# Seven-product scheme from the third column pair on, in a four-layer decoder trunk on one core

## The reference

```
def _swiglu(x, w13, w2):
    h = x @ w13                       # (512, 1024) @ (1024, 2 * 2816)
    g, u = jnp.split(h, 2, axis=-1)
    return (jax.nn.silu(g) * u) @ w2  # (512, 2816) @ (2816, 1024)
```

## Time and profile before

| what | value |
|---|---|
| time, median of 3 runs | 2118.74 us (2118.0 to 2120.76) |
| profiled execution, its own time | 2117.91 us |
| profiled execution, span from first to last instruction | 2116.0 us |
| granted TensorE clock, mean | 0.997 |
| PE matmul busy | 2093.9 us, 99% of the span, 14232 instructions |
| DVE busy | 1497.5 us, 71% |
| ACT busy | 915.3 us, 43% |
| POOL busy | 581.3 us, 27% |

### The profile page before, as it was taken

One profiled execution on the slowest core, in us unless ns is written; L12 is line 12 of the kernel. 1 busy time (PEld: TensorE's weight loads), 2 busy tenths in 40 slices (PEclk: granted clock), 3 DMA queues, 4 the chain that ended last, 5 costly groups with the idle time before them and its releaser, 6 DMA issues.

```text
span 2116.0 us, 37240 instructions
## 1 busy us (share of the span) xinstructions
PE 2093.9 (99%) x14232; PEld 1847.2 (87%) x14233; DVE 1497.5 (71%) x2106; ACT 915.3 (43%) x1662; POOL 581.3 (27%) x403
## 2 busy tenths in 40 slices
PE   9999999999999899999999999999999999999998
PEld 7777899998888689999888899988887778999987
DVE  3788688884379979888635888863638868888634
ACT  3455444443345134454323454442335454444422
POOL 0000146650030004666300366610000002666200
PEclk9999999999999999999999999999999999999999
DMA  6211333333233023334522233433332122334421
GB/s 219 70 50 50 94 109 101 101 109 129 92 110 100 23 70 110 101 101 115 176 96 64 80 100 103 116 122 99 101 89 61 60 78 73 100 110 111 125 94 60
DMA packets 256804, 204.65 MB, mean 97 GB/s; under 512 B 6272, under 2 KB 235776, under 8 KB 256656
## 3 DMA queue, kind: packets, MB, share of 16 engines
q1 hardware_dynamic: 252976, 189.42, 30.1%
q0 software_dynamic: 3680, 13.17, 1.9%
HBM read 200.47 MB, written 2.10 MB: 96 GB/s over the span
## 4 chain that ended last, share of the span: by engine, by line
PE 96%; DVE 2%; DMA 1%; ACT 1%; issue 0%; POOL 0%; DVEq 0%; POOLq 0%; SPq 0%; ACTq 0%
PE ps L1520 17%; PE ps L1522 17%; PE ps L1521 17%; PE ps L1599 12%; PE ps L1600 12%; PE ps L1601 12%; PE ps L1826 2%; PE ps L1854 2%; PE ps L1985 2%; PE ps L1641 1%; PE ps L1839 1%; PE ps L1830 1%; PE ps L2076 0%; DMA raw<-in_w 0%; PE ps L1652 0%
## 5 line engine op out<-in xcount | busy, mean ns | idle before, releaser
L986 DVE TENSOR_TENSOR w_lo<-raw,w_hi 128x1024 fp32r<-128x1024 f32 x188 | 233.4, 1247 | 317.4 <-ACT w_hi L609 316.6
L609 ACT ACTIVATE w_hi<-raw 128x1024 fp32r<-128x1024 f32 x188 | 195.5, 1056 | 345.3 <-PE ps L1522 336.1
L1599 PE MATMUL ps<-t_hi,w_hi 128*128 128x256 f32 x1216 | 344.3, 283 | 0.0
L1600 PE MATMUL ps<-t_lo,w_hi 128*128 128x256 f32 x1216 | 344.2, 283 | 0.0
L1601 PE MATMUL ps<-t_hi,w_lo 128*128 128x256 f32 x1216 | 344.2, 283 | 0.0
L678 ACT ACTIVATE w_hi<-raw 128x512 fp32r<-128x512 f32 (+1 forms) x304 | 224.2, 737 | 264.2 <-PE ps L1601 249.3
L1520 PE MATMUL ps<-w_hi,a_hi 128*128 128x512 f32 x832 | 326.3, 392 | 0.2
L1522 PE MATMUL ps<-w_hi,a_lo 128*128 128x512 f32 x832 | 324.0, 389 | 0.0
L1521 PE MATMUL ps<-w_lo,a_hi 128*128 128x512 f32 x832 | 323.9, 389 | 0.0
L1428 DVE TENSOR_TENSOR w_lo<-raw,w_hi 128x512 fp32r<-128x512 f32 (+1 forms) x304 | 281.6, 927 | 50.1 <-ACT w_hi L678 50.1
L1599 PE MATMUL ps<-xT_hi,w_hi 128*128 128x256 f32 x912 | 258.3, 283 | 0.0
(11 more groups left out here) (174 smaller groups left out, 4141.2 us busy)
## 6 DMA issues: line engine op xcount, KB each, us to landing
raw<-in_w SPq DMA_DIRECT2D x264, 512.0 KB, 4.0
raw<-in_wqkv SPq DMA_DIRECT2D x48, 512.0 KB, 3.7
raw<-in_pw SPq DMA_DIRECT2D x24, 512.0 KB, 4.3
raw<-in_wo SPq DMA_DIRECT2D x16, 512.0 KB, 3.4
ln_gb<-in_g POOLq DMA_DIRECT2D x8, 512.0 KB, 4.4
ln_gb<-in_b POOLq DMA_DIRECT2D x8, 512.0 KB, 5.7
x_nat<-in_x SPq DMA_DIRECT2D x4, 512.0 KB, 5.6
out<-x_nat SPq DMA_DIRECT2D x3, 512.0 KB, 2.6
```

The costliest lines, as they stand in the source:

```text
L609: nc.scalar.activation(weight_hi(u), raw[:, r, :], ACT.Copy).then_inc(w_hi_done, 1)
L986: nc.vector.tensor_tensor(weight_lo(u), raw[:, r, :], weight_hi(u).bitcast(f32), ALU.subtract).then_inc(w_lo_done, 1)
L1599: ms = [nc.tensor.matmul(dst, hi[:, at], x_hi, start=k == 0 and f in ("A11", "S1", "S2"), stop=False, skip_group_check=True), nc.tensor.ma ...
L1600: nc.tensor.matmul(dst, hi[:, at], x_lo, start=False, stop=False, skip_group_check=True),
```

## The change

Four things change, in each of the four stages "up".

1. `SEVEN_FROM` goes from 3 to 2. Pair 2 is no longer a plain pair, the scheme covers pairs 2 to 21 (20 of 22). On PE 48 matmuls over 512 tokens go and 84 over 256 tokens come.
2. On PE the first product, A11 of p = 0, is put ahead of unit 3, the last plain unit. Then come A12, S2, S1, S3.
3. `keep_first(0)` waits for unit 3 too, since its buffer lies in that unit's slot.
4. The low parts of the token sums are awaited one by one: S2 needs the first written (T2), S1 the second (T1), S3 the third (T3), A22 the fourth (T4). Before, S2 waited for all four. DVE and ACT make them in that order, with the splits of p = 0 between them; the fourth token sum is in a function of its own (`last_sum`).

```
-SEVEN_FROM, SEVEN_TO = 3, FC
+SEVEN_FROM, SEVEN_TO = 2, FC
...
-            order += [(p, f) for f in ("A11", "S2", "A12", "S1", "S3")]
+            order += [(p, f) for f in ("A11", "A12", "S2", "S1", "S3")]
...
                 act.wait_ge(form_used, used(i, p, "A11"))
+                if p == 0:
+                    act.wait_ge(w_used, u0 + 2 * SEVEN_FROM)
...
-                for k in range(AHEAD + 1, 2 * SEVEN_FROM):
-                    split_w(u0 + k)
+                split_w(u0 + AHEAD + 1)
+                form_high(0, G_A1)
                 activated(0)
+                form_high(0, G_S23)
+                for r in range(3):
+                    turned_hi(r)
+                keep_first(0)
+                form_high(0, G_S1)
                 activated(1)
...
-            split_w(u0 + 2 * SEVEN_FROM - 1)
-            for r in range(4):
-                turned_lo(r)
-            form_low(0, G_A1)
...
+            tokens_whole()
+            form_low(0, G_A1)
+            token_sums()
+            form_low(0, G_S23)
+            turned_lo(T2)
+            turned_lo(T1)
+            form_low(0, G_S1)
             gating(0)
-            token_sums()
...
+            turned_lo(T3)
+            make_u2(0)
+            last_sum()
+            gating(1)
             form_low(0, G_A22)
             form_low(0, G_S4)
...
+            turned_lo(T4)
...
                 elif f == "S2":
-                    pe.wait_ge(t_lo_done, 4 * (i + 1))
+                    pe.wait_ge(t_lo_done, 4 * i + 1)
...
-                for c in range(2, SEVEN_FROM):
-                    pair(c)
                 order = form_order()
-                for p, f in order[:-2]:
+                product(*order[0])
+                up_unit(u0 + AHEAD + 1, bank + AHEAD + 1)
+                for p, f in order[1:-2]:
                     product(p, f)
```

More of the change, by code:

```diff
@@ L700, in up @@
             if bias is None:
-                for k in range(AHEAD + 1, 2 * SEVEN_FROM):
-                    split_w(u0 + k)
+                split_w(u0 + AHEAD + 1)
+                form_high(0, G_A1)
                 activated(0)
-                activated(1)
-                for r in range(4):
[L706 to L709, removed]
+                form_high(0, G_S23)
[3 more added lines that the diff above has]
+                form_high(0, G_S1)
+                activated(1)
                 form_high(0, G_A22)
                 form_high(0, G_S4)
-                form_high(0, G_S1)
-                keep_first(0)
+                turned_hi(3)
                 first_tokens(0)
@@ L1397, in token_sums @@
             def token_sums():
-                r22, r12, r11, r21 = (t_raw[:, r, :, :] for r in range(4))
+                r22, r12, r11 = (t_raw[:, r, :, :] for r in range(3))
                 dve.wait_ge(t_raw_done, 4 * i + 2)
@@ L1405, in token_sums, with last_sum @@
                 nc.vector.tensor_tensor(r11, r22, r11, ALU.add).then_inc(t_sum_done, 1)
+            def last_sum():
+                r11, r21 = (t_raw[:, r, :, :] for r in (2, 3))
                 dve.wait_ge(t_raw_done, 4 * i + 4)
@@ L1469, in _ @@
             split_w(u0 + AHEAD + 1)
[L1470 to L1475, removed]
-            gating(0)
-            token_sums()
-            split_w(u0 + 2 * SEVEN_FROM - 1)
-            for r in range(4):
-                turned_lo(r)
-            form_low(0, G_A1)
-            gating(SEVEN_FROM - 2)
-            form_low(0, G_S23)
+            tokens_whole()
[5 more added lines that the diff above has]
+            form_low(0, G_S1)
+            gating(0)
+            turned_lo(T3)
+            make_u2(0)
+            last_sum()
+            gating(1)
             form_low(0, G_A22)
             form_low(0, G_S4)
-            gating(SEVEN_FROM - 1)
-            form_low(0, G_S1)
-            make_u2(0)
+            turned_lo(T4)
             for p in range(1, SEVENS):
@@ L1561, in up @@
                 up_columns(u0 + k, bank + k, second_half(b)).then_inc(w_used, 1)
-            up_unit(u0 + AHEAD + 1, bank + AHEAD + 1)
             X, Y, Z = seven_bank(i), seven_bank(i) + 1, seven_bank(i) + 2
@@ L1582, in product @@
                 elif f == "S2":
-                    pe.wait_ge(t_lo_done, 4 * (i + 1))
+                    pe.wait_ge(t_lo_done, 4 * i + 1)
                     if p:
                         pe.wait_ge(c21_done, m)
-                elif f == "S1" and p:
-                    pe.wait_ge(c12_done, m)
+                elif f == "S1":
+                    pe.wait_ge(t_lo_done, 4 * i + 2)
+                    if p:
+                        pe.wait_ge(c12_done, m)
                 elif f == "S3":
+                    pe.wait_ge(t_lo_done, 4 * i + 3)
                     pe.wait_ge(u2_done, m + 1)
                 elif f == "A22":
+                    pe.wait_ge(t_lo_done, 4 * (i + 1))
                     pe.wait_ge(u3_done, m + 1)
```

## The result

The changed kernel takes 2151.02 us (median of 4 runs, 2150.06 to 2153.0), the kernel before 2118.91 in the same session (4 runs, 2118.0 to 2120.76). The ratio is 1.0155, with a 95% interval of 1.0143 to 1.0168: 1.55% slower, where 2148 us (1.4%) was forecast. The profiled execution took 2150.42 us, its span is 2148.6 us, the mean granted clock 0.994 (2117.91, 2116.0 and 0.997 before).

The account below looks back on a forecast made before the run. PE bounds the kernel with DVE right behind in each stage head; a layer loses 7.7 + 0.6 - 0.82 - 0.1 = 7.35 us, four 29.4, on 2117.9 gives 2147.3, shown as 2148 us; range 2138 to 2160.

Parts of the forecast that it names:

- DVE's list: Stage head, layer 0: DVE's instructions up to the low part for A11 of p = 1 end at 292.3 us.
- the count of seven meetings: Stage head: seven POOL instructions take turns with DVE instructions having both inputs in SBUF, 1.07 us each, 7.5 in all.
- The waits: Stage head: PE loses 7.7 us a layer, at A11, A12, S1, S3 and A11 of p = 1.
- The wait at S3 of p = 1: Second scheme pair: DVE late once more, at `make_u2` before S3, 0.6 us a layer (0 to 0.7).
- The gain: PE, pair 2: a seven-product pair takes 10.08 us instead of 10.90, saving 0.82 a layer, 3.3 over four.
- the likeliest case: Whole kernel: DVE's list makes PE wait in each stage head, no clock fall; 2148 us, 1.4% slower, 77 in 100.
- the rival that had it at 15 in 100: Clock falls in the new hole, about 2 us after the last matmul; 1.5 us a layer, 2154; 15 in 100.
- against it: the holes sit between dense products: Argument against the clock falling: small transposes stood ahead of the convolution's stop, dense products surround the new 3.8 us hole.
- The sum: A layer: 7.7 + 0.6 - 0.82 - 0.1 = 7.35 us; four layers 29.4.
- Not slower: Stage head: POOL turns cost nothing, DVE's list ends at 284.8, A11 of p = 1 on time; 2118; 4 in 100.
- Lateness in every pair: All 20 scheme pairs: `make_u2` stays 0.6 us late, 46 us more, 2193; 4 in 100.
- Signs named ahead: New profile: A11 1.2 us late, 0.7 idle around unit 3, 3 to 4 at DVE's low part, period 10.08.

Follow-up runs that it names:

- experiment 6: Changed kernel with POOL's first three weight sums of a stage started earlier, ahead of the last tokens' low part; 2143.16 us, ratio 1.0112.
- experiment 3: Changed kernel with S2 ahead of A12 again on PE (A11, unit 3, S2, A12, S1, S3); 2152.27 us, ratio 1.0155.
- experiment 5: Changed kernel with T3's low part made twice on DVE, one more 128x1024 instruction in each layer's head; 2157.77 us, ratio 1.018.
- experiment 1: Changed kernel with fifteen unread 512-token matmuls filling PE's hole ahead of A11 of p = 1; 2146.84 us, ratio 1.0133.
- Experiment 11: experiment 10's kernel with `make_u2` of p = 1 ahead of the gating of p = 0 on DVE; 2116.1 us, ratio 0.9987.
- experiment 9: experiment 7's kernel with unit 3 ahead of A11, S2 ahead of A12, p = 0 splits in order of need, `keep_first(0)` later; 2122.82 us, ratio 1.0018.
- experiment 10: Changed kernel with the changes of experiment 6 and experiment 9 together; 2116.64 us, ratio 0.9991.
- experiment 8: The control: kernel before with whole tokens copied by ACT from `ps` instead of DVE's four additions; 2118.45 us, ratio 0.9996.
- experiment 4: Changed kernel with the weight split for A11 of p = 1 moved ahead of A22's, S4's and T4's low parts; 2151.62 us, ratio 1.0159.
- experiment 7: Changed kernel with whole tokens copied by ACT from `ps`, replacing DVE's four additions, token sums ahead of A1's low part; 2136.82 us, ratio 1.0083.
- experiment 2: Kernel before with only `SEVEN_FROM` set to 2, old order and one wait for all four token low parts; 2150.87 us, ratio 1.0149.

## Why the prediction was right, point by point

**DVE's list.** Forecast to end at 292.3, it ended at 291.98, in a stage that began 0.37 us earlier (262.62 against 262.99 of the earlier trace rows). The prices by kind, the count of seven meetings and the place of the first three (on the token additions) all hold; a meeting cost 7.6 / 7 = 1.09 instead of 1.07. That a meeting costs DVE time when both its operands come from SBUF, and none otherwise, was read off one trace; experiment 6 shows it with the same POOL instructions moved. The Trainium skill (SBUF — State Buffer, "SBUF: two separate sides") says why: the pair of ports that the two engines share is locked for a whole instruction, and the loser waits until it is done. The rows agree in kind, 2.2 to 2.3 us for DVE and 2.1 to 2.3 for POOL where alone they take 1.21 and 1.30. They don't agree to the end: a turn of both takes 0.2 to 0.3 us less than the 2.5 of the two together.

**The waits.** Forecast 7.7 a layer in p = 0 and at A11 of p = 1: 1.2, 0.7, 1.4, 0.6, 3.8. Measured 1.23, 0.79, 1.16, 0.61, 3.67, 7.46. That they are one list's lateness and not five causes is shown by experiments 3 and 5. The wait at S3 of p = 1, forecast 0.6 with 0 as the lower end, came as 0.18 in one layer and not at all in three. Against the kernel after that is 0.4 to 0.6 too much a layer; experiment 1, with the clock up in all layers, has 0.38 to 0.48. So the term was mis-sized by 0.1 to 0.2 a layer there, and in layers 0, 1 and 3 the slow clock, which the forecast left out, hid the rest.

**The gain.** 0.82 us a layer is what the periods give. Experiment 11 has it without waits and comes out 2.4 us, 0.6 a layer, under before; its four stages, measured as below, are 0.66 to 0.84 shorter. Restarts, 0.07 us each at four or five places of a layer, were not in the sum, and make up for part of what was too much at S3.

**The clock.** This term was mis-sized: the likeliest case had nothing for it. It fell in three layers of four, and the rival that had it at 15 in 100 was right in these three that it falls and on its price (1.5 us a layer, measured 1.4 to 1.5). It had the fall inside the hole, about 2 us after the last matmul as in the earlier trace rows, and it came after PE's restart. By the trace the slow matmuls took 4.3 us, by experiment 1 the net price is 3.4 to 4.2. The step that failed is "against it: the holes sit between dense products": dense work around a hole of this length did not keep the clock. The two cases stood as alternatives, 2148 and 2154, and the median of 2151.02 lies between them. That the likeliest case is only 3 us off has some luck in it: the clock was missing from it, and the wait at S3, which the low clock hid, was in it.

**The sum.** From the end of the last `xT_lo` to the end of the last gating, DVE's marks of a stage, the four stages grew by 8.33, 8.00, 7.22 and 8.59 us. The forecast was 7.35, and layer 2, where the clock held, has 7.22. That match is in part luck too: 0.4 too much at S3, against restarts (0.35) and a loss of 0.22 that were not in the sum. The other three have 0.8 to 1.4 more. Together 32.1, of the 32.6 by which the span grew; of the rest, the stretch ahead of layer 0's stage became 0.38 shorter and the one ahead of layer 1's 0.88 longer, and why stays open. Counted from PE: waits 29.6, clock 4.3, restarts and two single losses of 0.22 in layers 2 and 3 (not explained) 1.7, less 4 x (0.82 + 0.1), 31.9.

**The other rivals.** "Not slower" named the point from which it decides, 0.9 us of waits a layer. Experiments 9 and 10 stand on its two sides: 1.8 us a layer gave 1.0018, 0.5 gave 0.9991. "Lateness in every pair" was wrong, since the window at 305 to 345 is full.

**Signs named ahead.** A11 of p = 0 about 1.2 late, `over_hi<-ps` behind unit 3 with 0.7 idle, 3 to 4 us at the low part of L1433, DVE without idle time, a period of 10.08: all are there. Of the four additions, "2.3 us for three of them" is 7.92 in all, three meetings on four instructions.

## What to carry to other kernels

A stage where the bound engine is busy to the last tenth can still sit right beside a second list that ends just in time. Before giving the bound engine less work there, walk the other engine's list to the instruction that it must deliver next, with the meetings of engines that share a port counted as instructions of their own. Time taken from that list is worth nothing while it is on time (experiment 8); when it is late, time added is paid in full (experiment 5) and time taken is nearly all won (experiment 6, 1.9 of 2.2). Reordering moved the waits but didn't shorten them while the list had no idle time (experiments 3 and 4). As soon as instructions were gone, DVE stood idle for ACT (experiment 7), and then the order was worth more than half of the waits that were left (experiment 9). So look for idle time in the late engine's list again after each step.

## What the runs showed of the hardware

In the kernel after, the clock fell behind holes of 3.7 us only once PE was dense again, 0.4 to 1.4 us after its start. It isn't always so: behind holes of the same length it fell inside the hole in layer 3 of experiment 3 and in layer 1 of experiments 5 and 6. For experiment 6, where PE stopped at 831.3 and started again at 834.81 (length, busy, granted clock, DMA):

```profile
833.00:834.50 1.50, 0.00 (x0) 0.62 0.42 121
```

Behind the hole of 5.76 us in experiment 2 the first matmul is slow already (0.55 us long instead of 0.36), and in the convolution the clock fell inside the stop. It is also no function of the hole alone. Over the 11 profiles of 20 pairs (the kernel after and the experiments but the control), the 44 heads of a stage divide so: longest wait 3.1 us or more (24 heads), a fall in 23; 2.3 us (four heads of experiment 4), a fall in two; 1.1 us or less (12 heads of experiments 9 to 11), none; the four with the filler, none. A fall behind a hole of 3.7 us took another 1.4 to 1.5 us in the kernel after (15 or 16 x 0.093), and up to 2.5 in experiments 3, 5 and 6 (27, 26 and 23 matmuls).

DVE and POOL take turns at the cost of a whole instruction, 1.1 us here, whether the one is a sum, a low part or a token addition. But an operation with one operand in `ps` pays nothing (experiment 6: 1.22 and 1.23 us beside POOL's 1.30), so the same three POOL instructions cost 2.2 us less when they start 3.4 us earlier.
